# Modulation, splits and first input products of a hybrid block in four parts, with the conditioning row sent through DRAM

## The reference, cut to what matters

```python
D_MODEL = 2048; SEQ = 256; N_MEM = 256
def first_block(x, c, ada_w, ada_b, norm_mix_g, ...):
    c_act = jax.nn.silu(c)                       # (1, 2048)
    mod = c_act @ ada_w[layer] + ada_b[layer]    # (1, 6 * 2048)
    sh1, sc1, g1, sh2, sc2, g2 = jnp.split(mod, 6, axis=-1)
    u = rms_norm(h, norm_mix_g[layer]) * (1.0 + sc1) + sh1
    h = h + g1 * hybrid_mixer(u, w_in[layer], ...)     # proj = u @ w_in, then four kinds of attention
    ...                                          # the SwiGLU half, with sh2, sc2, g2
def hybrid_layer(x, mem, ...):                   # the second block
    m = rms_norm_2(mem, mem_norm_g)
    mk, mv = jnp.split(m @ w_mem_kv, 2, axis=-1)
    ...
```

## Time and profile before

| | us |
|---|---|
| median of 3 runs | 2514.92 (2513.91 to 2520.58) |
| the profiled execution | 2520.33, of which span 2518.5 |
| PE busy | 2457.3 (98% of the span) |
| DVE busy | 1523.9 (61%) |
| ACT busy | 1021.3 (41%) |
| POOL busy | 124.0 (5%) |
| share of the chain that ended last | PE 83%, DMA 8%, DVE 7% |

### The profile page before, as it was taken

How to read it: one execution, slowest core, us unless ns; L and a number is a source line. 1 busy time by engine, 2 the same in 40 slices (tenths; PEclk the granted TensorE clock), 3 DMA queues, 4 the chain that set the end, 5 groups by cost and what they waited for, 6 DMA issues and landing times.

```text
span 2518.5 us, 34620 instructions
## 1 busy us (share of the span) xinstructions
PE 2457.3 (98%) x14904; PEld 1994.6 (79%) x14904; DVE 1523.9 (61%) x1784; ACT 1021.3 (41%) x1255; POOL 124.0 (5%) x228
## 2 busy tenths in 40 slices
PE   6999999999899999999998999999999999999999
PEld 3479987977788888888887888878888777777887
DVE  5576678787755556444544756546954455457764
ACT  2132335565443343333434444543644333334332
POOL 1001111110000000000000000011000000000000
PEclk9998999999999999999999999999999999999999
DMA  9987996656466666656555544466655333336654
GB/s 412 426 301 291 348 338 231 243 187 217 183 228 239 234 229 240 200 189 228 189 195 223 228 166 156 172 225 211 214 190 184 135 135 127 135 135 226 254 183 165
DMA packets 86649, 554.70 MB, mean 220 GB/s; under 512 B 9910, under 2 KB 10070, under 8 KB 33376
## 3 DMA queue, kind: packets, MB, share of 16 engines
q1 hardware_dynamic: 56384, 403.26, 43.9%
q0 software_dynamic: 30112, 149.21, 16.1%
HBM read 535.66 MB, written 13.65 MB: 218 GB/s over the span
## 4 chain that ended last, share of the span: by engine, by line
PE 83%; DMA 8%; DVE 7%; issue 1%; ACT 1%; POOL 0%; SPq 0%; DVEq 0%; ACTq 0%; POOLq 0%
PE psum L2258 40%; PE psum L1031 25%; DMA weights<-in_ada_early 4%; DMA arena<-in_loads 3%; PE psum L2487 2%; PE psum L2273 2%; PE psum L2484 2%; PE psum L2241 1%; DVE arena L2651 1%; PE psum L1233 1%; PE psum L2401 1%; PE psum L1240 1%; PE psum L1242 1%; DVE weights L2639 1%; DVE unit_low L2627 1%
## 5 line engine op out<-in xcount | busy, mean ns | idle before, releaser
L1936 ACT ACTIVATE unit_high<-weights 128x1024 fp32r<-128x1024 f32 (+1 forms) x509 | 720.1, 1428 | 1086.6 <-PE psum L2258 610.5
L2627 DVE TENSOR_TENSOR unit_low<-weights,unit_high 128x2048 fp32r<-128x2048 f32 x219 | 501.6, 2291 | 430.0 <-ACT unit_high L1936 429.9
L1445 DVE TENSOR_TENSOR unit_low<-weights,unit_high 128x1024 fp32r<-128x1024 f32 x240 | 289.5, 1221 | 169.6 <-ACT unit_high L1936 169.3
L2258 PE MATMUL psum<-unit_low,z_high 128*128 128x512 f32 x1152 | 286.5, 391 | 3.7 <-DVE unit_low L2627 3.7
L2258 PE MATMUL psum<-unit_high,z_high 128*128 128x512 f32 x1152 | 288.8, 393 | 0.0
L2258 PE MATMUL psum<-unit_high,z_low 128*128 128x512 f32 x1152 | 284.6, 389 | 0.0
L1031 PE MATMUL psum<-unit_high,z_high 128*128 128x512 f32 x960 | 272.4, 401 | 0.0
L1031 PE MATMUL psum<-unit_low,z_high 128*128 128x512 f32 x960 | 266.6, 395 | 1.3 <-DVE unit_low L1445 1.3
L1031 PE MATMUL psum<-unit_high,z_low 128*128 128x512 f32 x960 | 266.4, 395 | 0.0
L2258 PEld LDWEIGHTS psum<-unit_low,z_high 128*128 128x128 f32 x1152 | 217.2, 189 | 49.6 <-DVE unit_low L2627 4.5
L2258 PEld LDWEIGHTS psum<-unit_high,z_low 128*128 128x128 f32 x1152 | 216.3, 188 | 45.0
(11 more groups left out here) (432 smaller groups left out, 2791.2 us busy)
## 6 DMA issues: line engine op xcount, KB each, us to landing
weights<-in_loads SPq DMA_DIRECT2D x380, 1024.0 KB, 4.7
arena<-in_loads POOLq DMA_DIRECT2D x88, 512.0 KB, 6.0
arena<-in_ada_early POOLq DMA_DIRECT2D x8, 2048.0 KB, 22.0
weights<-in_ada_early POOLq DMA_DIRECT2D x8, 2048.0 KB, 24.6
xn<-in_loads POOLq DMA_DIRECT2D x32, 512.0 KB, 5.5
gates_kept<-h POOLq DMA_DIRECT2D x12, 512.0 KB, 3.7
arena<-gates_kept POOLq DMA_DIRECT2D x12, 512.0 KB, 8.8
arena<-in_b_rows POOLq DMA_DIRECT2D x10, 512.0 KB, 7.0
```

Source lines behind the costliest of these rows:

```text
L1445: ins = V.tensor_tensor(ring_lo[:, g % RING, c], ring[:, g % RING, c], unit_hi[:, g % 2, c].bitcast(F32), ALU.subtract)
L1936: return nc.scalar.activation(out_, in_, ACT.Copy, scale=scale)
L2258: ins = mm(psum[:, bank + m, 0:width], xk[:, m * P:(m + 1) * P], w[:, k, 0:width], start=(first and i % 8 in (0, 4) and part == 0), stop=( ...
L2627: V.tensor_tensor(ring_lo[:, g % RING], ring[:, g % RING], unit_hi[:, g % 2].bitcast(F32), ALU.subtract)\
```

## The change

1. **The conditioning row by way of DRAM.** `c_diag`, the four products by ones and ACT's copy are gone. POOL writes the 128 x 16 values of `c_act` to a row of 2048 in DRAM (element by element, since neighbours in DRAM lie on different partitions), waits for it, and reads the row back to all partitions (1 MiB) into `c_start`. The early blocks stand behind both. The later copy of the row to DRAM is gone, and the reload before the last pieces reads the row to all partitions.
2. **32 blocks one by one, by parts.** The order is by quarters of the width: the 4 blocks of shift and the 4 of scale for the first 512 columns, then the next. Loads are 1 MiB, into four buffers in `arena`; `early2` is gone, so `Wb[:, 1]` is free for the splits from the start. The load of x stands ahead of block 9, and x is normalized after block 11. From block 20 on DVE reads the row from `h[:, 0]`.
3. **Splits by parts.** `scale_col` is made per quarter. DVE makes the low parts of quarters 0, 1 and 2 after blocks 22, 25 and 28.
4. **PE's order.** 4 rounds of mem's transposes stand ahead of unit 0, the other 4 behind units 0 and 1. x is transposed behind memory units 11, 13 and 15 and behind input unit 2. Units of the first two loads (positions 0 and 1) alternate quarter by quarter, and so does `STREAM`. `cmp_hidden` stands behind unit 10.
5. **Pieces.** They begin at unit 8 instead of 4: 56 in 23 slots instead of 27.

```diff
-STREAM = ([(PLAN["w_in"][0] + i, q) for i in W_IN_ORDER for q in range(4)]
+STREAM = ([(PLAN["w_in"][0] + i, q) for q in range(4) for i in W_IN_ORDER[:2]]
+          + [(PLAN["w_in"][0] + i, q) for i in W_IN_ORDER[2:] for q in range(4)]
...
-SLOT_PIECE = [range(k * 56 // 27, (k + 1) * 56 // 27) for k in range(27)] + [range(0)]
+SLOT_PIECE = [range(k * 56 // 23, (k + 1) * 56 // 23) for k in range(23)] + [range(0)]
+EARLY = [(n, b) for q in range(4) for n in (q, 4 + q) for b in range(4)]
...
-        c_dram = nc.dram_tensor("c_kept", (P, D), F32, kind="Internal").ap()
+        c_dram = nc.dram_tensor("c_kept", (1, D), F32, kind="Internal").ap()
...
# POOL
+            pool.wait_ge(s_["c_row"], 1)
+            pool.dma_start(c_dram[0].rearrange("(k p) -> p k", p=P), c_act[:], allow_slow_non_contiguous=True)\
+                .then_inc(s_["c_kept"], 16)
+            pool.wait_ge(s_["c_kept"], 16)
+            pool.dma_start(c_start, c_dram.broadcast_to([P, D])).then_inc(s_["c_kept"], 16)
             pool.wait_ge(s_["mem_in1"], 16)
+            for i, (n, b) in enumerate(EARLY):
+                if i == 9:
                     pool.dma_start(h[:], A["x"].rearrange("(m p) n -> p m n", p=P)).then_inc(s_["x_in"], 16)
+                if i >= 4:
+                    pool.wait_ge(s_["early_used"], i - 3)
+                pool.dma_start(early[:, i % 4], A["ada_early"][n, b // 2][:, b % 2 * D:(b % 2 + 1) * D])\
+                    .then_inc(s_[f"ada_in{i % 4}"], 16)
...
-            pool.wait_ge(s_["c_row"], 4)
-            pool.dma_start(c_dram, h[:, 0]).then_inc(s_["c_kept"], 16)
...
# ACT
+            act.wait_ge(s_["early_used"], C_MOVED)
+            act.wait_ge(s_["c_row"], 2)
+            split_quarter(0)
+            split_quarter(1)
             high(0)
-            act.wait_ge(s_["mod_ready"], 1)
-            act.wait_ge(s_["c_row"], 4)
-            split_transposes(KT // 2, z_hi, scale_col, mod[:, 0:16])
             high(1)
             read_mem(3)
+            split_quarter(2)
+            high(2)
+            high(3)
+            split_quarter(3)
+            for g in range(4, 8):
+                high(g)
...
# PE
-            for b in range(4):
-                ins = mm(psum[:, b], ones, c_diag[:, 4 * b:4 * b + 4].rearrange("p k n -> p (k n)"), start=True, stop=True)
...
-            transposes(xn, KT)
+            transposes(xn, KT // 2)
+            for u in range(16):
+                if u < 4:
+                    pe.wait_ge(s_["tr_free"], 2 * u + 2)
+                mem_unit(u)
+                if u < 2:
+                    transposes(xn, KT // 4, 8 + 4 * u)
+                if u == 11:
                     pe.wait_ge(s_["norm_ready"], 4)
+                if u in (11, 13, 15):
+                    transposes(xn, KT // 4, 2 * (u - 11))
...
+            for q in range(4):
+                if q == 0:
+                    pe.wait_ge(s_["acc_free"], acc + 1)
+                pe.wait_ge(s_["tr_free"], KT // 2 + 2 * q + 2)
+                unit_features(2 * q, 4 * q, 0, q == 0, q == 3)
+                if q == 0:
+                    pe.wait_ge(s_["acc_free"], acc + 2)
+                if q == 1:
+                    transposes(xn, KT // 4, 12)
+                unit(2 * q + 1, 4 * q, 2, q == 0, q == 3, z_hi, z_lo)
...
# DVE
-            V.tensor_tensor(c_diag, ident.unsqueeze(1).broadcast_to([P, KT, P]),
...
+            for i in range(len(EARLY)):
+                if i == C_MOVED:
+                    dve.wait_ge(s_["c_row"], 2)
+                ada_early(i)
+                if i == 11:
                     rms(1)
                     scale_tokens(h)
+                if i % 8 == 7:
+                    mixer_scale(i // 8)
+                if i in (22, 25, 28):
+                    dve.wait_ge(s_["mod_ready"], (i - 22) // 3 + 1)
+                    split_affine(mod[:, 0:16], 4 * (i - 22) // 3)
+                if i == 28:
+                    low(0)
+                    low(1)
+                if i == 29:
+                    low(2)
+            low(3)
+            dve.wait_ge(s_["mod_ready"], 4)
+            split_affine(mod[:, 0:16], 12)
+            for g in range(4, 8):
+                low(g)
```

More of the change, by code:

```diff
@@ L510, in hybrid_blocks @@
         block = ctx.enter_context(nc.Block())
-        def early_of(n):
-            return (early2 if n % 2 else early), 2 * (n % 2), n // 2
         small0 = small(2)
@@ L2082, in projected @@
                 copy(tm[:, :, (i - 8) * CH:(i - 7) * CH], src).then_inc(s_["acc_free"], 1)
-            for pos in range(N_DENSE):
+            for pos in range(2, N_DENSE):
                 for q in range(4):
-                    if q == 2 and pos:
+                    if pos == 2 and q < 2:
+                        projected(q)
+                    if q == 2 and pos > 2:
                         projected(pos - 1)
-                    if pos:
-                        high(4 * pos + q)
+                    high(4 * pos + q)
                     if (pos, q) == (2, 3):
@@ L2351, in _ @@
             base, acc = PLAN["w_in"][0], FIRST_ACC["w_in"]
-            pe.wait_ge(s_["acc_free"], acc + 1)
-            woven(xn, lambda c: None, 0, lambda g, q: unit_features(g, 4 * q, 0, q == 0, q == 3), made=1)
-            for pos in range(1, N_DENSE):
+            for q in range(4):
[8 more added lines that the diff above has]
+                unit(2 * q + 1, 4 * q, 2, q == 0, q == 3, z_hi, z_lo)
+            for pos in range(2, N_DENSE):
                 pe.wait_ge(s_["acc_free"], acc + pos + 1)
@@ L2655, in _ @@
             step(V.tensor_scalar(c_act[:], c_act[:], 0.5, 0.5, ALU.mult, ALU.add)); step.wait()
[L2656 to L2659 removed]
+            V.tensor_tensor(c_act[:], c_act[:], v_("c"), ALU.mult).then_inc(s_["c_row"], 1)
             lv = v_("lam").rearrange("p (i d) -> p i d", i=4)
@@ L2725, in gelu_out @@
                 V.tensor_tensor(z[5], z[4], z[0], ALU.mult).then_inc(s_["gelu_ready"], 1)
-            dve.wait_ge(s_["c_row"], 4)
-            beside = {(1, 3): blocks, (2, 3): fox_logits, (3, 1): gelu_in, (3, 3): fox_logs, (4, 0): gelu_out}
-            for pos in range(1, N_DENSE):
+            beside = {(2, 1): blocks, (2, 3): fox_logits, (3, 1): gelu_in, (3, 3): fox_logs, (4, 0): gelu_out}
+            for pos in range(2, N_DENSE):
                 for q in range(4):
-                    slot = 4 * (pos - 1) + q
+                    slot = 4 * (pos - 2) + q
                     low(4 * pos + q)
```

87 lines of the change are left out of this document (24 added, 63 removed).

## The result

| | before | changed |
|---|---|---|
| median, us | 2516.71 (2509.47 to 2522.64, 8 runs) | 2527.83 (2523.35 to 2536.22, 8 runs) |
| ratio | | 1.0049, 95% interval 1.0031 to 1.0067 |
| profiled execution, us | 2520.33 | 2523.35 |

The changed kernel is 11 us slower. In a second set of rounds it took 2527.15 us against 2515.47, ratio 1.0057 (1.0040 to 1.0073). The forecast was 2517.5 and "the same" the likeliest; the time lies within the range of 2503 to 2529, but the kernel is slower, clear of noise.

A forecast was written before the change was run, and what follows sets the result against it. The prediction took PE and DMA both to be full in the opening, and nearly so in the dense stage. A gain of 4.7 us and a cost of 7.5 made +2.8, so 2517.5 us on the median, range 2503 to 2529.

The forecast's parts named there:

- PE's start: Opening: memory unit 0 begins at about 22.5 us instead of 31.17, with less work ahead of it.
- up to 8 us later: Opening: if the write delays mem, PE starts this much later, nearly all covered by its 6.5 us lead at u = 13.
- The write stops DMA for 8.5 us: Opening, about 9.5 to 18 us: during the row's element-wise write DMA moves next to nothing for 8.5 us (bounds 0 and 10).
- the first rival: Opening: the element-wise write disturbs nobody, quarter 2 and low(0) end 10.8 us earlier, 2506.7 us; chance 0.17.
- PE waits 8 us at u = 13: After memory unit 13: PE waits from 122.0 to 130.1 us for block 22 and quarter 0's transposes.
- Gain 4.7 us at unit 8: End of the opening: unit 8 begins at 198.3 us instead of 203.03.
- a sign of being wrong: Unit 8 beginning before 190 or after 204 us would show the prediction wrong.
- Dense stage, cost 7.5 us: Behind unit 12: five more pieces of 0.524 MB at 351 GB/s cost 7.5 us.
- the sum -4.7 + 7.5: Whole kernel: the gain up to unit 8 and the dense stage's cost make +2.8 us.
- PE's wait for `low(0)`: First input unit: PE waits 2.5 us in its third part, low(0) being done at 154.1 us.
- The traced execution: Whole kernel: 2520.33 us profiled would become 2523.1; lying 5.4 above the median, it makes 2517.7 on the median.
- The slow rival: Dense stage: pieces bound by their round trip, five more cost 14.4 us, +9.7 in all, 2524.6 us; chance 0.25.

The follow-up runs named there:

- a_again: The changed kernel once more, unchanged, for a second trace and five more timed executions: 2527.15 us, ratio to before 1.0057.
- slots27: The changed kernel with part 5 undone, its 56 pieces again behind units 4 to 30 in 27 slots: 2529.04 us, ratio to before 1.0059.
- row_dense: The changed kernel with the row turned by PE and written to DRAM in 16 rows of 512 bytes: 2515.66 us, ratio to before 0.9990.
- half_pieces: row_dense with pieces 3 to 55 loading half of their columns (output differs): 2502.55 us, ratio to before 0.9945.
- moved8: row_dense with 8 of the 56 dense-stage pieces moved into attention: 2509.11 us, ratio to before 0.9970.
- late_write: row_dense plus an element-wise write of 2048 values ahead of piece 21 that nobody waits for: 2525.46 us, ratio to before 1.0040.
- low_early: row_dense with low(0) on DVE behind block 25 instead of 28: 2515.44 us, ratio to before 0.9998.
- after_moved8: The changed kernel, element-wise write kept, with 8 of the 56 pieces moved into attention: 2520.8 us, ratio to before 1.0016.
- part1_only: The kernel before with part 1 alone, the row written element by element and read back: 2529.77 us, ratio to before 1.0050.
- old_dense: The kernel before with the row by DRAM in 16 rows of 512 bytes, old order kept: 2516.64 us, ratio to before 1.0009.

## Why the prediction was wrong, step by step

*PE's start:* right, 22.27 in a_again for 22.5. In the first trace mem came late (33.21), a case the prediction had named, with "up to 8 us later" where 11 came.

*The write stops DMA for 8.5 us:* right, 8.8 us missing, and the first rival (nobody disturbed) is out. With it goes the 2.0 us plus bytes of the Trainium skill's page "DMA: Bandwidth & Descriptors", section "Anatomy of one DMA — SWDGE (gpsimd) path": 15.5 us were measured for 8 KB. The prediction said that the trace's 10.8 us bears out one descriptor per element. It bears out only that the fit is too low: in the first 30 us the profile counts 175 packets under 512 bytes with the write and 160 before, so single elements are not seen in it.

*PE waits 8 us at u = 13:* the place was right, the size was not: 12.7 us in a_again, none in the first trace. Block 22 was counted done at 126.8. It was at 126.1 in the first trace, where PE came so late that it was free, and at 131.7 in a_again.

*Gain 4.7 us at unit 8:* 4.3 between the first traces, but 0.8 between the means of the two traces of each kernel (201.4 against 202.2). The 204.1 of a_again passes the 204 that the prediction had called a sign of being wrong.

*Dense stage, cost 7.5 us:* from unit 8 to attention 172.6 and 168.4 us, before 165.6 and 167.7: 3.9 more on the mean. The reason given was five more pieces behind unit 8. slots27, with fewer pieces there, was no faster, so their place is not what counts.

*The step that failed* is the sum -4.7 + 7.5: it carries what is gained up to unit 8 to the end and adds a fixed cost for the dense stage. Take the prediction's two halves, the write's price (its forecast less the first rival, 10.8 us) and all the rest (8.0 us faster: 15.5 gained by unit 8, 7.5 given back).

The rest is worth 2.5 us at the end, not 8.0 (row_dense, 0.9990; its interval reaches from 6.0 faster to 1.3 slower). Of the 15.5 us the traces have 10.2: unit 8 begins at 192.0 on the mean of the four traces with row_dense's order up to there (row_dense, half_pieces, moved8, late_write: 190.8 to 193.1), against 202.2 before. Most of what is missing is one term, PE's wait for `low(0)`, 5.02 us in row_dense for the 2.5 of the forecast, with slow products behind it (3.52 us instead of 2.08). But putting that term right would not have put the time right. low_early has no such wait, begins unit 8 at 184.7, 17.5 us ahead of before, and takes the same time as before (0.9998). What PE gained up to unit 8 came back as waits in the dense stage, 19.5 us of them behind unit 8 in that trace against 5.4 and 7.3 before; the prediction had no term for this.

The write's price is not so forgiven. Up to unit 8 it is 10.0 us (202.0 on the mean of the three traces with it, against 192.0), close to the 10.8. At the end four pairs measure it: 15.8 us (changed kernel and row_dense), 11.6 (after_moved8 and moved8), 12.6 (late_write and row_dense, with the write in the dense stage) and 10.3 (part1_only and old_dense), 12.6 on the mean. Each is uncertain by 4 to 5 us, so that it is more than the forecast's 10.8 is not shown, and that the 15.8 holds a further debt of bytes, paid in the dense stage, is likely and not shown. What is shown is that a stall of the transfers is still there at the end, where a gain of PE's is not. 15.8 less 2.5 is the 13.3 us that the mean ratio 1.0053 gives.

*The traced execution:* the sum, +2.8 us, is what the traces show (+3.0), in part by luck: the first trace meets both terms (4.3 and 7.0 us for 4.7 and 7.5) by another path, a late PE and no wait at u = 13. On the means of two traces both terms are near half their size or less, 0.8 and 3.9. The median differs by 11. Subtracting the 5.4 us by which one execution lay above its median took it as the same for both versions. Both traces of before lie above its medians (3.6 and 4.9 us), and those of the changed kernel below (4.5 and 1.0); an error of this kind is as large as the effect, and no trace of before holds a median execution.

*The slow rival*, pieces bound by their round trip, has the side right. Whether it has the mechanism is open: half_pieces halved the bytes and also shortened a landing.

## What to carry to other kernels

In a stage that waits for its loads, count all the bytes that must have moved by its end, in one account (here 129.8 to 131.4 MB before attention in the 15 traces with whole pieces in the dense stage): a stall anywhere before was still there at the end, and time gained by reordering engines came back as waits, while bytes moved behind the stage's end paid, less what they cost there. Do not write single elements to DRAM while transfers are wanted, even a few hundred; let PE turn the values first. Measure how far a trace lies from its median, for each version, before a sum of a few us is built on it; and look for the stretch that takes the same time in every trace, since the rest holds the difference.

## What the hardware showed that was not expected

- An element-wise write of 256 values (1 KB) slows the other transfers nearly as long as one of 2048: 71 to 96 GB/s for 9 us against 74 to 93. In 16 rows of 512 bytes the rate stays at 421 to 434 GB/s. The Trainium skill, page "DMA: Bandwidth & Descriptors", section "Specifications", puts the smallest transfer at line rate at 512 B; the traces agree in so far as rows of that size hold nothing up (the row itself is 8 KB of 6.4 MB there), and that section does not say what smaller ones do to others.
- During that write in the first trace the DMA share reads 0.76 to 1.53 at 74 to 281 GB/s: it tells how long packets took, not what they moved.
- Beside the write of 8 KB a 1 MiB transfer that was issued 4 us before it took 19.41 us to landing in one execution, and 8.7 in another.
